# A four-layer transformer and a hybrid block on one core: boundaries between stages reordered, the last norm pair fused, first tiles split finer

## What is computed

```python
for i in range(4):
    x = layer_norm(ALPHA * x + 0.5 * swiglu(x, ffn1_w13[i], ffn1_w2[i]), ln_g[i, 0], ln_b[i, 0])
    y = (dsa, fox, mla, dsa)[i](x)      # sparse, forgetting, latent, sparse attention
    x = layer_norm(ALPHA * x + y, ln_g[i, 1], ln_b[i, 1])
    x = layer_norm(ALPHA * x + 0.5 * swiglu(x, ffn2_w13[i], ffn2_w2[i]), ln_g[i, 2], ln_b[i, 2])
# second block
h = rms_norm_2(x, norm_mix)
qa, ka, va, u, qm, km, vm, gates = split_in(h @ w_in)
ya = swa_attention(qa, ka, va, sinks, slopes) @ w_o_swa
z = gelu(s5_ssm(u, ...)) @ w_glu
yb = (z[..., :512] * sigmoid(z[..., 512:])) @ w_o_ssm
yc = moba_attention(qm, km, vm, slopes) @ w_o_moba
g = sigmoid(gates)
x = x + (g[..., :1024] * ya + g[..., 1024:2048] * yb + g[..., 2048:] * yc) @ w_out
h = rms_norm_2(x, norm_ffn)
x = x + square(relu(h @ w_ff1)) @ w_ff2
out = rms_norm_2(x, norm_final)
```

## Time and profile before

| what | value |
| --- | --- |
| median of three runs | 2610.25 us (2608.78 to 2610.42) |
| profiled execution, its own time | 2613.03 us |
| its span | 2611.2 us |
| TensorE busy | 2501.6 us, 13221 matmuls |
| VectorE busy | 1511.8 us |
| ScalarE busy | 1187.9 us |
| mean granted clock of TensorE | 0.982 |

### The profile page before, as it was taken

How to read it: one execution, slowest core, us unless ns; L and a number is a source line. 1 busy time by engine, 2 the same in 40 slices (tenths; PEclk the granted TensorE clock), 3 DMA queues, 4 the chain that set the end, 5 groups by cost and what they waited for, 6 DMA issues and landing times. The chain is left out here.

```text
span 2611.2 us, 32687 instructions
## 1 busy us (share of the span) xinstructions
PE 2501.6 (96%) x13221; PEld 2104.4 (81%) x13221; DVE 1511.8 (58%) x2149; ACT 1187.9 (45%) x1493; POOL 402.3 (15%) x467
## 2 busy tenths in 40 slices
PE   8999999999999999999889999999999988999998
PEld 6888778888888788888777888887878867898897
DVE  5546664464455654654566446447675556897455
ACT  4534454444454544444455444444554454444443
POOL 0002210000001100000130000002259502670000
PEclk9999999999999999999999999999999999999999
DMA  7554335555544465555225555555335531345453
GB/s 237 186 186 150 120 130 187 193 164 191 193 147 130 130 193 188 167 192 184 88 99 175 183 190 170 185 181 161 114 125 183 192 129 58 104 130 179 160 192 123
DMA packets 314966, 417.04 MB, mean 160 GB/s; under 512 B 18761, under 2 KB 273090, under 8 KB 314818
## 3 DMA queue, kind: packets, MB, share of 16 engines
q1 hardware_dynamic: 314818, 414.96, 49.5%
HBM read 413.87 MB, written 1.05 MB: 159 GB/s over the span
## 5 line engine op out<-in xcount | busy, mean ns | idle before, releaser
L463 DVE TENSOR_TENSOR wlo<-raw,whi 128x2048 fp32r<-128x2048 f32 (+3 forms) x402 | 918.7, 2291 | 626.4 <-ACT whi L455 625.7
L455 ACT ACTIVATE whi<-raw 128x2048 fp32r<-128x2048 f32 (+3 forms) x402 | 747.4, 1867 | 449.6 <-DMA raw<-in_ffn_w_dram 398.4
L576 PE MATMUL ps<-whi,xh 128*128 128x512 f32 (+4 forms) x2056 | 784.1, 381 | 20.9 <-DVE wlo L463 9.2
L577 PE MATMUL ps<-wlo,xh 128*128 128x512 f32 (+4 forms) x2056 | 773.4, 376 | 0.0
L578 PE MATMUL ps<-whi,xl 128*128 128x512 f32 (+4 forms) x2056 | 772.8, 376 | 0.0
L576 PEld LDWEIGHTS ps<-whi,xh 128*128 128x128 f32 x2056 | 394.8, 192 | 97.8 <-issue 15.0
L578 PEld LDWEIGHTS ps<-whi,xl 128*128 128x128 f32 x2056 | 394.5, 192 | 68.3
L577 PEld LDWEIGHTS ps<-wlo,xh 128*128 128x128 f32 x2056 | 395.4, 192 | 64.8
L576 PE MATMUL ps<-whi,oh 128*128 128x512 f32 x960 | 387.1, 403 | 3.4 <-DVE wlo L463 2.4
L578 PE MATMUL ps<-whi,ol 128*128 128x512 f32 x960 | 375.2, 391 | 0.0
L577 PE MATMUL ps<-wlo,oh 128*128 128x512 f32 x960 | 374.3, 390 | 0.0
(11 more groups left out here) (295 smaller groups left out, 2373.2 us busy)
## 6 DMA issues: line engine op xcount, KB each, us to landing
raw<-in_ffn_w_dram SPq DMA_DIRECT2D x352, 512.0 KB, 4.8
raw<-in_ffn_w_dram SPq DMA_DIRECT2D x88, 1024.0 KB, 4.9
raw<-in_w_ff_dram SPq DMA_DIRECT2D x32, 1024.0 KB, 5.1
raw<-in_w_out_dram SPq DMA_DIRECT2D x20, 1024.0 KB, 4.9
raw<-in_w_in_dram SPq DMA_DIRECT2D x20, 1024.0 KB, 5.1
raw<-in_dsa_w_in_dram SPq DMA_DIRECT2D x32, 512.0 KB, 4.4
raw<-in_dsa_w_in_dram SPq DMA_DIRECT2D x12, 1024.0 KB, 5.1
raw<-in_fox_w_in_dram SPq DMA_DIRECT2D x16, 512.0 KB, 4.7
```

The source lines that it names most:

```text
L455: act.activation(hi(u)[:, 0:w], raw[:, (slot[u] + 1) % SLOTS, 0:w], ACT.Copy).then_inc(sem("hi_ready"), 1)
L463: dve.tensor_tensor(lo(u)[:, 0:w], raw[:, (slot[u] + 1) % SLOTS, 0:w], hi(u)[:, 0:w].bitcast(F32), ALU.subtract).then_inc(sem("lo_ready"), 1)
L576: pe.matmul(o, ah, bh, start=start, stop=False, skip_group_check=True)
L577: pe.matmul(o, ah, bl, start=False, stop=False, skip_group_check=True)
```

## The change

**What it does.**

1. `init`: the first unit is split in four pieces of 512 columns, and TensorE waits for each piece by itself.
2. The second rows are turned behind all twelve matmuls of the second unit in every `ffn`, in `index` and in `forget`, and behind the second unit in `latent`.
3. VectorE's split at the end of a feed-forward moves behind the first rows' turn where `ahead` is 3; in front of `latent` one more unit is split between the first and the second rows.
4. `index` and dsa: a split moves into the third top-k round and one into the sixth; the second group's `narrow` tiles, their copies and the values' move stand ahead of the first scores, and the third group's first `wide` tiles around the second scores.
5. mla: at i == 3 one more output unit is split.
6. The stages "bare" norm, `lift` and root-mean-square norm become one norm stage: gain and shift come by two DMAs of 512 KB as rows, VectorE applies them in row layout, ScalarE sums the squares. The residual `cx` is made later from 16 transposes of `xn` (in col, behind `first_wide(1, 0)`) and two copies.
7. col: sines and cosines are computed in another order, keys are copied by VectorE, units are split one earlier, `wide(1, 0, 0)` stands between the first and the second scores, `ssm_input` and `turned_qk` stand earlier in their steps.
8. `ssm`: the chunks are spread otherwise, and unit u + 15 is split ahead of the last gate multiplies.
9. `oproj2` and `ff`: the first rows are turned behind the first half of the columns; the first two up-units are computed with tokens as rows, for the first rows ahead of the second rows' turn, their squares are turned by 8 transposes, and the order of the weights in the ring follows.

The diff, cut:

```diff
-        plan.append(dict(kind="norm", g=3 * layer + 2, eps=4 * LN_EPS,
-                         c=2 * ALPHA, bare=layer == DEPTH - 1))
+        if layer < DEPTH - 1:
+            plan.append(dict(kind="norm", g=3 * layer + 2, eps=4 * LN_EPS, c=2 * ALPHA))
     plan += [
-        dict(kind="lift"),
-        dict(kind="norm", g=12, eps=RMS_EPS, rms=True),
+        dict(kind="norm", g=12, eps=RMS_EPS, rms=True, lift=4 * LN_EPS),
...
-    return min(60, 4 + 7 * (i + 1) // 2)
+    return 4 + 3 * (i + 1) + 2 * ((i + 3) // 4)
...
-                last = u + 3 * q + 4 + i % 2
+                last = u + 3 * q + 4 + i % 2 + (i == 3)
...
+                if u == sines_u + 6:
+                    sp.wait_ge(sem("unit_used"), sines_u)
+                    for dst, name in ((lift_gain, "ln_g"), (lift_shift, "ln_b")):
+                        sp.dma_start(dst, a[name][DEPTH - 1, 2:3, :].broadcast_to([P, DM])).then_inc(sem("lift_in"), 16)
                 load(sp, u, units[u])
...
+                if "lift" in st:
+                    split_hi(act, u + 1)
+                    for t in range(NT):
+                        act.wait_ge(sem("lift_made"), 2 * t + 2)
+                        act.activation(xT[:, :, t * P:(t + 1) * P], xn[:, t, :].rearrange("p (k s) -> p k s", k=KT), ACT.Square,
+                                       accum_out=sm[:, t, 0:1]).then_inc(sem("lift_sum"), 1)
...
+                        act.activation(lifted(t, 0), xn[:, t, 0:512], ACT.Identity, scale=rstd[:, t, 1:2]).then_inc(sem("xn_act"), 1)
+                        turned(t)
+                        split_hi(act, u + 2)
...
+                    if st["next"]["kind"] == "latent":
+                        split_hi(act, u + 2)
...
+                        if i == 15:
+                            split_hi(act, u + 15)
...
-                    turned(0, lambda: split_lo(dve, 0))
+                    def first_low():
+
+                        for n in range(4):
+                            c = slice(512 * n, 512 * n + 512)
+                            dve.wait_ge(sem("hi_ready" if n == 3 else "first_hi"), 1 if n == 3 else n + 1)
+                            dve.tensor_tensor(lo(0)[:, c], raw[:, (slot[0] + 1) % SLOTS, c], hi(0)[:, c].bitcast(F32),
+                                              ALU.subtract).then_inc(sem("lo_ready" if n == 3 else "first_lo"), 1)
+                        split_to["lo"] = 1
+
+                    turned(0, first_low)
...
+                    dve.wait_ge(sem("lift_in"), 32)
+                    dve.wait_ge(sem("angles"), 1)
+                    first_stats(0)
+                    spread(0)
+                    centred(0)
+                    made(0)
+                    split_lo_half(dve, u + 1, 0)
+                    mean_square(0)
+                    first_stats(1)
+                    scaled(0)
+                    split_lo_half(dve, u + 1, 1)
+                    spread(1)
+                    turned(0, lambda: centred(1))
+                    made(1)
+                    split_lo_half(dve, u + 2, 0)
+                    mean_square(1)
+                    scaled(1)
+                    split_lo_half(dve, u + 2, 1)
+                    turned(1)
+                elif kind == "norm":
                     first_stats(0)
                     stats(0)
-                    if prev["kind"] == "oproj":
+                    if prev["kind"] == "oproj" or prev["kind"] == "ffn" and ahead[u] == 3:
+                        split_lo(dve, u)
                         turned(0, lambda: split_lo(dve, u + 1))
                         first_stats(1)
                     else:
...
+                    if st["next"]["kind"] == "latent":
+                        split_lo(dve, u + 2)
                     turned(1)
...
-                    split_lo(dve, D(FIT - 2) + ahead[u])
+                    if ahead[st["end"]] == 2:
+                        split_lo(dve, D(FIT - 2) + ahead[u])
...
-                    split_lo(dve, u + 5 + ahead[u])
                     dve.wait_ge(sem("ix_acc"), 8 * n + 8)
                     ch.link(dve.tensor_tensor(acc[:, :], acc[:, :], causal[:, :], ALU.add))
                     ch.wait()
                     for r in range(TOPK // 8):
+                        if r == 2:
+                            split_lo(dve, u + 5 + ahead[u])
+                        if r == 5:
+                            split_lo(dve, u + 8)
...
+                        if n == 15:
+                            split_lo(dve, u + 15)
...
+                    if u == 0:
+                        for n in range(3):
+                            pe.wait_ge(sem("first_lo"), n + 1)
+                            up(0, 0, 0, n)
+                        unit_ready(pe, A(0))
+                        up(0, 0, 0, 3)
+                    else:
+                        unit_ready(pe, A(0))
+                        up(0, 0, 0)
                     x_ready(0, 1)
                     unit_ready(pe, A(0) + 1)
-                    if st["w"]:
-                        up(0, 1, 0).then_inc(sem("h0_done"), 1)
+                    up(0, 1, 0).then_inc(sem("h0_done"), 1)
+                    if u:
                         residual(pe, b("cx_ready"), 0, range(4))
-                        turn_norm(prev, 1)
-                        pe.wait_ge(sem("xt_dve"), b("xt_dve") - 1)
-                        residual(pe, b("cx_ready"), 0, range(4, 8))
-                    else:
-                        up(0, 1, 0, 0)
-                        turn_norm(prev, 1)
-                        for k in (1, 2, 3):
-                            last = up(0, 1, 0, k)
-                        last.then_inc(sem("h0_done"), 1)
-                        pe.wait_ge(sem("xt_dve"), b("xt_dve") - 1)
-                        residual(pe, b("cx_ready"), 0)
+                    turn_norm(prev, 1)
+                    pe.wait_ge(sem("xt_dve"), b("xt_dve") - 1)
+                    residual(pe, b("cx_ready"), 0, range(4 if u else 0, 8))
                     for m in range(2):
                         x_ready(1, m)
...
+                    if "lift" not in st["next"]:
+                        turn_norm(st["next"], 0)
                     used(by_columns(lambda c, ns: dn(e, 1, c, ns)))
...
-                                if t == 0 and m and k == 0:
+                                if t == 0 and m and k == 3:
                                     turn_norm(prev, 1)
...
-                            elif m == 0:
+                            elif m == 1:
                                 turn_norm(prev, 1)
...
+                        turn_norm(prev, 0)
+                        first_wide(0, 0)
+                        first_wide(0, 1)
+                        unit_ready(pe, u + 2)
+                        for k in range(KT):
+                            if k == 4:
+                                turn_norm(prev, 1)
+                            token_major(pe, ps[:, 2, 0:256], u + 2, 0, 256, 0, range(KT), 256, only=k)
+                        first_wide(1, 0)
...
+                            for k in range(KT):
+                                last = pe.transpose(ps[:, 4 + 2 * t + k // 4, k % 4 * P:(k % 4 + 1) * P], xn[:, t, k * P:(k + 1) * P], ident[:, :])
+                            last.then_inc(sem("lift_turned"), 1)
+                        first_wide(1, 1)
                         narrow(0, 1)
+                        pe.wait_ge(sem("lift_cx"), 2)
                         turn(0)
                         turn(1)
                         scores(0)
...
                         if st["mix"] == "dsa":
+                            narrow(1, 0)
+                            narrow(1, 1)
                             scores(0)
...
+                            if col and i == 0:
+                                wide(1, 0, 0)
+                            if st["mix"] == "dsa" and i == 0:
+                                wide(2, 0, 0)
                             if i + 1 < NP:
                                 scores(i + 1)
                             if col and i == 0:
-                                wide(1, 0, 0)
                                 wide(1, 0, 1)
-                            if not col and q < last_q:
+                            if not col and q < last_q and (i or st["mix"] != "dsa"):
                                 narrow(q + 1, 0)
                                 narrow(q + 1, 1)
...
+                            if st["mix"] == "dsa" and i == 0:
+                                wide(2, 0, 1)
                             values(i)
...
-                            if t and m == 3:
-                                turn_norm(st["next"], 0)
...
+                                last = by_columns(lambda c, ns: down(pe, u + m, (xh, xl), 2 * m, t, c, ns),
+                                                  (lambda: turn_norm(st["next"], 0)) if t else None)
...
+                    x_ready(0, 1)
+                    rows(0, 0)
+                    turn_norm(prev, 1)
+                    rows(1, 0)
```

(11 more changed lines are left out.)

317 lines of the change are left out of this document (201 added, 116 removed).

## The result

| kernel | median (lowest to highest), runs | ratio to before [95%] | profiled run, span |
| --- | --- | --- | --- |
| before, same chip | 2609.75 us (2608.78 to 2610.42), 4 | 1 | |
| the change | 2596.9 us (2595.42 to 2598.12), 4 | 0.9947 [0.9934, 0.9959] | 2598.04, 2596.3 |

The change is faster by 12.9 us, some 0.5%. The forecast was 31.8; 2596.9 lies outside its range of 2568 to 2592.

What follows compares the result with a forecast made beforehand. TensorE was taken as busy 96% of the span, leaving only waits and half-clock stretches to win. Terms summed to 31.8 us off the profiled 2613.0: 2581.2 profiled, 2578.5 as a median, range 2568 to 2592.

Steps and rivals of the forecast that it cites:

- the term "+5.0": ssm: splitting the next-stage tile ahead of two gate multiplies removes a 2.07 wait and 1.7 of half clock; ends 2 and 7.
- The prediction's own sign, a granted clock of 1.00 from 2350 to 2360: Listed among the signs that the forecast is right: TensorE at full clock from 2350 to 2360 us.
- The rival of the side engines: VectorE and GpSimd set ssm's end, so ssm begins early and waits: 5.0 + 6 us lost, 2590; 16%.
- the term "2.9 - 2.05 + 0.15 = -1.0": Each index stage and forget: second rows' 2.9 us chain loses nine matmuls' 2.05 cover, plus 0.15 lost overlap; costs 1.0.
- "+1.9" without the -1.0: Top-k stages: filling the 5.17 wait for scores, with a new 3.7 wait, leaves +0.9 each after index's -1.0.
- Start, "+1.0": First tile in quarters: first matmul 2.9 us earlier, near 10.7, of which 1.0 is kept; ends 0 and 2.
- the three feed-forward boundaries: Second rows' late turn brings waits of 0.4, 0.9, 0.8, less shortened earlier waits: -1.3 each, -3.9 for three.
- latent and mla: Earlier splits remove waits of 2.74 and 2.37 and some half clock: +5.1 and +2.0.
- lift: Two norms and the lift become one: first col matmul 8.9 us earlier; with col +14.3 together, ends 10 and 17.
- the last feed-forward: Later turns remove 4.3 of 7.7 waited and 3.8 of some 5 lost to clock: +7.2; ends 4 and 10.
- The clock turned on it: Rival: late turns make the clock fall at all seven boundaries (36 us) and 19 of the gain goes: 2633; 2%.
- The late second `xn`: Rival: the new split delays second statistics, so the second turn waits at all seven boundaries, 7 times 1.7: 2590 to 2592; 8%.

Runs made afterwards that it cites:

- x3: The change, but TensorE turns the second rows early again in index, forget and first feed-forwards, VectorE's new order kept: 2597.19 us.
- x7: The kernel before with the mla edit alone (one more output unit split at i == 3): 2608.47 us.
- x2: The change with ssm's early split of unit u + 15 taken back, the new spread of the chunks kept: 2596.28 us.
- x1: The change with dsa's split (low half of the third group's first unit) moved ahead of the first scores' mask work: 2582.84 us.
- x5: The change with the first weight tile split whole again instead of in quarters: 2597.67 us.
- x12: The change with the last feed-forward and the turn in oproj2 as before: 2604.06 us.
- x6: x2 with the ssm chunks also spread as before, so the change with its whole ssm part undone: 2591.31 us.
- x8: x2 with VectorE's ys(3) moved ahead of the second split (u + 16) in ssm: 2592.83 us.
- x11: The change with latent's part taken back (third unit split behind the second rows, these turned behind the first unit): 2601.32 us.

## Why the prediction was wrong

**ssm, the term "+5.0"; measured -3.3.** This step failed in its sign. It priced what the early split takes off TensorE, a 2.07 wait and half clock behind it, and gave VectorE's side one cautious sentence, that it is busy 89.75 of 94 us. Two things were missing. The other edit of ssm, the spread of the chunks, was put at nothing, and it is the one that moves VectorE's split to right behind the last scan; the split call ahead of the gates, to which the term gives the whole gain, moves nothing on VectorE. And GpSimd: there the split lands beside the four multiplies on which TensorE's last products wait, and each 2.29 of split is added. The sum comes 8.58 after the scan instead of 6.51, TensorE waits 2.66 and 2.49 where it waited 2.07, and a further fall of the clock takes 1.7. The prediction's own sign, a granted clock of 1.00 from 2350 to 2360, did not come: it was 0.85. The rival of the side engines named this rule and saw one half of it, a split 0.96 longer. It had 16% and 2590 us, and it placed the loss in an early start that only waits, where the start's gain was kept and the end lost. The other half of the pair, how long GpSimd's 2.66 multiply is beside that split, stood in the trace of before and is not in the prediction.

**index, the term "2.9 - 2.05 + 0.15 = -1.0"; measured -2.86 and -4.58.** The chain from the second turn's start to its `xl` takes 2.98 us (212.51 to 215.49), as forecast 2.9; 1.07 of it is the turn itself, and the nine matmuls' 2.05 had covered the rest. Without them the wait is not the remainder, 0.85, but that whole rest, 1.91, and it is 1.91 at all three places where the rows have no residual (215.49, and in the same way 755.80 and 1779.34). The wait ahead of the first turn shrinks from 0.97 to 0.22, which pays 0.75 back and which the term had left out. The two errors nearly cancel: 1.91 - 0.75 = 1.16, and at `forget`, where the clock took no more than before, the step came out at -1.2 for -1.0. That is luck of the sum. What the term lacked was the clock behind the new wait. It took 1.7 more at the first `index` (0.79 in 214 to 222; 1.91 - 0.75 + 1.7 = 2.86, measured 45.00 - 42.14 = 2.86) and 3.4 more at the second (0.89 over the 45 us from 1760, against 0.96 over the 40 us from 1759 in before; 1.91 - 0.88 + 3.4 = 4.4). A part of this is the draw of the two traces; over all traces the step costs 2.5. Nor is the missing cover the whole cause: x3 gives it back and waits 1.85 all the same, for VectorE's split stands ahead of the second rows' statistics.

**dsa, "+1.9" without the -1.0; measured +0.2** from the first scores to the last turned probability in the first one (108.89 to 108.73) **and -0.2** in the second (108.39 to 108.60). The wait was foreseen: some 3.7 behind the mask work, measured 4.04 and 4.29. That VectorE's 3.92 idle us ahead of it was the obvious place for the split, I did not see. What failed is the clock, which I had set off against the old fall as equal. The clock behind the two waits looks equal, 0.73 over ten us in the kernel before and 0.69 in the change:

```profile
267.00:277.00 10.00, 9.16 (x60) 8.51 (x61) 5.71 (x25) 4.62 (x11) 4.44 (x10) 0.73 0.01 2
```

```profile
275.00:285.00 10.00, 9.89 (x38) 7.46 (x38) 3.32 (x17) 3.20 (x4) 4.45 (x10) 0.69 0.00 1
```

But in the kernel before the fall begins inside the old wait: the granted clock is 0.89 in 264 to 266 and 0.50 in 266 to 268, and TensorE, idle until 267.84, loses nothing by the first 2.3 us of it. In the change it begins only at the wait's end (0.59 in 274 to 276, the wait ends at 275.11), and nearly all of it falls on matmuls. The falls end in 272 to 274 (0.90) and in 280 to 282 (0.70). From these figures I estimate 2.3 us lost before and 3.1 after. So 1.1 was won between the two waits (5.17 to 4.04), where I had 1.5, and the clock took some 0.8 of it back. Nor does the term's own sum come out: 1.5 less the 1.0 of `index`, less an overlap, is not 0.9 but under 0.5, so 0.4 of each 1.9 had no source.

**Start, "+1.0"; measured +0.2.** The first quarter at 10.7 was 10.84. Its 2.9 us became 2.05 at the first gate, and the late turn took some 1.4 of that. The sum had ends of 0 and 2, so this is a size, not a step.

**Right for the reasons given:** the three feed-forward boundaries, waits 0.39, 0.87 and 0.81 for 0.39, 0.87 and 0.83, -1.45 each for -1.3; latent and mla, +7.2 for 7.1 (4.8 and 2.4 for 5.1 and 2.0), with no wait over 0.72 left in 1262 to 1285; lift, its first col matmul 9.2 earlier against the last gate for 8.9, with 2.13 and 2.75 waited in the fused norm's chain (lift and col of before took 129.0 in its own trace and 126.6 in x7's, against 113.6); the last feed-forward, +8.7 for 7.2, where the waits left are 1.08, 1.57 and 0.50 for 0.9, 2.0 and 0.5, and the clock came back fully and not in part. The size of the last one leans on the profiled execution: x7, with the same feed-forward as before, took 232.2 and not 235.7 there, against which the gain is 5.2.

**The rivals.** The clock turned on it at two of the seven boundaries, for some 5 us of 36. The late second `xn` is real, as x3's 1.85 shows, but not at 1.7 seven times. The rest of the chance sat on gains; no rival joined a collision in ssm with a dearer `index` and a dsa that gives nothing, which is what happened.

## What to carry over

When a wait is filled by moving work, price what the removed cover hid: the new wait is the whole rest of the chain behind the last thing that TensorE itself does for it (here 1.91), not what was left over beside the cover, and behind it comes the clock. Where a fall of the clock lies counts as well as whether it comes: inside a wait it costs nothing. When a VectorE operation with two SBUF operands moves, be it only because a neighbour has moved, look first at which GpSimd operation it will lie beside, and whether TensorE is waiting for that one; here their times add. And a new wait is a place to look for an idle engine: an idle stretch just ahead of it, as VectorE's 3.92, is room for the operation that is waited for.

## What was unexpected of the hardware

The fall of TensorE's clock isn't decided by the wait alone. In the change and in x2 the code at `index` is the same and so is the wait, 1.91 (TensorE's row of x2, then its stretch; that of the change is above):

```profile
214.90 0.50 PE L597 MATMUL ps<-whi,xh 128*128 128x512 f32 x1 [1.91 <-DVE xl L1352]
```

```profile
214.00:222.00 8.00, 7.10 (x39) 6.12 (x39) 6.10 (x5) 6.71 (x9) 0.79 (x2) 1.00 0.38 115
```

The granted clock is 0.79 in one and 1.00 in the other, with the whole program 0.6 us earlier. Of the eight traces with this code and this wait, four have 0.79 in 214 to 222 (the change, x1, x5, x12) and four 1.00 (x2, x6, x8, x11); the wait ends between 214.82 and 216.91 in the first and between 214.90 and 215.38 in the second, so the place in time doesn't part them. The same last feed-forward of the kernel before took 235.7 us in its own trace and 232.2 in x7's, and 22 runs of before on one chip lie between 2603.87 and 2615.36. The Trainium skill (TensorE: Matmul & The Clock Gate, "Part 1: The HAM clock gate (the "warmup" mystery)") says that the number of matmuls at half clock at a kernel's start varies from run to run; here the same is seen in the middle of a program, behind waits near 2 us. Such waits should be priced with a fall as a chance and not as a certainty. Why the clock of the kernel before is 0.68 in 225 to 235, where TensorE waits for nothing, no run here has settled. So a part of 2 or 3 us that is read from one trace of each kernel, as in the table of marks, needs a second trace before it is believed.
